# Down projections by Strassen: which of VectorE and GpSimd forms the sums of activations and weights

## What is computed

```python
D_MODEL, SEQ, DEPTH = 1024, 1024, 2
D_FF = 2816
ALPHA = (2.0 * DEPTH) ** 0.25

def swiglu(x, w_gu, w_down):
    gate, up = jnp.split(x @ w_gu, 2, axis=-1)
    return (jax.nn.silu(gate) * up) @ w_down

x = layer_norm(ALPHA * h + swiglu(h, ffn_w_gu[l], ffn_w_down[l]), ln_g[l, 1], ln_b[l, 1])
```

## Time and profile before

| what | value |
|---|---|
| median of three runs | 3269.45 us |
| the profiled execution, its own time | 3274.18 us |
| its span | 3272.5 us |
| TensorE busy (matmul) | 2939.8 us, 90% |
| VectorE busy | 1775.2 us, 54% |
| ScalarE busy | 1204.3 us, 37% |
| GpSimd busy | 1040.3 us, 32% |
| first to last matmul of the steps in `ffn0d` | 1659.4 to 1927.1 us |
| first to last matmul of the steps in `ffn1d` | 2986.7 to 3244.1 us |

### The profile page before, as it was taken

The page is one execution under the profiler, slowest core; times in us unless marked ns, Lnnn a source line. Parts: engine busy times, 40 slices in busy tenths (PEclk is TensorE's granted clock), DMA queues, the critical chain, the costliest instruction groups (busy, mean ns, idle before and its releaser), DMA issues. The chain is left out here.

```text
span 3272.5 us, 50986 instructions
## 1 busy us (share of the span) xinstructions
PE 2939.8 (90%) x18874; PEld 2460.4 (75%) x18893; DVE 1775.2 (54%) x3186; ACT 1204.3 (37%) x2655; POOL 1040.3 (32%) x1097
## 2 busy tenths in 40 slices
PE   7999999678999869999989969869996999998995
PEld 7889777354566569999977759836664999997784
DVE  2168443484898463333359873324546333334988
ACT  2222543433555443333333441114444333333342
POOL 2200222440111024444346534400001444443555
PEclk8999887788999989999999979959998999999998
DMA  4211102443110022222173432230001222226343
GB/s 124 74 41 42 27 27 76 135 125 101 48 39 27 20 65 80 80 80 80 54 244 105 162 103 40 66 112 23 27 27 53 79 80 80 80 67 207 120 160 119
DMA packets 269998, 269.61 MB, mean 82 GB/s; under 512 B 61779, under 2 KB 197158, under 8 KB 269734
## 3 DMA queue, kind: packets, MB, share of 16 engines
q1 hardware_dynamic: 263254, 255.57, 25.1%
q0 software_dynamic: 6512, 10.89, 1.1%
HBM read 212.24 MB, written 55.89 MB: 82 GB/s over the span
## 5 line engine op out<-in xcount | busy, mean ns | idle before, releaser
L2228 PE MATMUL ffn0u_ps<-ffn0u_x_hi,ffn0u_whi 128*128 128x272 f32 x1232 | 358.8, 291 | 20.4 <-DVE ffn0u_wlo L2331 10.6
L2228 PE MATMUL ffn1u_ps<-ffn1u_x_hi,ffn1u_whi 128*128 128x272 f32 x1232 | 358.4, 291 | 20.0 <-DVE ffn1u_wlo L2331 10.9
L2228 PE MATMUL ffn0u_ps<-ffn0u_x_hi,ffn0u_wlo 128*128 128x272 f32 x1232 | 356.4, 289 | 0.0
L2228 PE MATMUL ffn1u_ps<-ffn1u_x_hi,ffn1u_wlo 128*128 128x272 f32 x1232 | 356.2, 289 | 0.0
L221 PE MATMUL ine_ps<-ine_w_hi,ine_x_hi 128*128 128x256 f32 (+2 forms) x864 | 262.0, 303 | 5.2 <-DVE ine_w_lo L237 5.0
L2228 PEld LDWEIGHTS ffn0u_ps<-ffn0u_x_hi,ffn0u_whi 128*128 128x128 f32 x1232 | 234.6, 190 | 22.5 <-DVE ffn0u_wlo L2331 21.2
L2228 PEld LDWEIGHTS ffn1u_ps<-ffn1u_x_hi,ffn1u_whi 128*128 128x128 f32 x1232 | 234.2, 190 | 22.2 <-DVE ffn1u_wlo L2331 20.9
L221 PE MATMUL ine_ps<-ine_w_hi,ine_x_lo 128*128 128x256 f32 (+2 forms) x864 | 249.4, 289 | 0.0
L221 PE MATMUL ine_ps<-ine_w_lo,ine_x_hi 128*128 128x256 f32 (+2 forms) x864 | 248.9, 288 | 0.0
L2228 PEld LDWEIGHTS ffn0u_ps<-ffn0u_x_hi,ffn0u_wlo 128*128 128x128 f32 x1232 | 234.4, 190 | 0.0
L2228 PEld LDWEIGHTS ffn1u_ps<-ffn1u_x_hi,ffn1u_wlo 128*128 128x128 f32 x1232 | 234.4, 190 | 0.0
(11 more groups left out here) (559 smaller groups left out, 7902.5 us busy)
## 6 DMA issues: line engine op xcount, KB each, us to landing
ffn0u_raw<-in_ffn_w_gu_dram SPq DMA_DIRECT2D x44, 512.0 KB, 5.1
ffn0d_w<-in_ffn_w_down_dram SPq DMA_DIRECT2D x88, 256.0 KB, 2.9
ffn1u_raw<-in_ffn_w_gu_dram SPq DMA_DIRECT2D x44, 512.0 KB, 5.4
ffn1d_w<-in_ffn_w_down_dram SPq DMA_DIRECT2D x88, 256.0 KB, 3.0
scratch_a<-ffn0u_u SPq DMA_DIRECT2D x44, 272.0 KB, 2.1
scratch_a<-ffn1u_u SPq DMA_DIRECT2D x44, 272.0 KB, 2.1
aT<-scratch_a SPq DMA_DIRECT2D x8, 1024.0 KB, 10.8
aT<-scratch_a SPq DMA_DIRECT2D x10, 768.0 KB, 9.2
```

The source lines that it names most:

```text
L2228: last = nc.tensor.matmul(ps[:, bank + h, 0:TOK2], wp, xp, start=(begins and k == 0 and n == 0), stop=(k == KH - 1 and n == 2), skip_group ...
```

## The change

VectorE now makes all 55 sums of activations, and the sums of weights of products 0 and 4 (22), so one sum in every step. GpSimd keeps the sums of weights of products 2, 3 and 6 (33). VectorE's sums for step n + 1 stand ahead of the low parts of step n; ahead of step 0 stand those of step 0 and of step 1. Semaphores are renamed and counted to match.

```diff
     def dve_sums_a(n):
-        return n in a_sum_at and n in w_sum_at and n % KH2 % 2 == 0
+        return n in a_sum_at
+
+    def dve_sums_w(n):
+        return n in w_sum_at and n not in a_sum_at
+
+    w_sum_count, w_made = {}, {True: 0, False: 0}
+    for n in w_sum_steps:
+        w_made[dve_sums_w(n)] += 1
+        w_sum_count[n] = w_made[dve_sums_w(n)]
...
-        def sum_w(eng, op, n):
+        def sum_w(eng, op, n, done):
             slot, f = raw_at[n] % RW, FACTOR_B[n // KH2]
             eng.wait_ge(w_in[slot], w_in_count[n])
             second = raw2[:, pair_at[n] % 2, :] if n in pair_at else b22(n % KH2)
-            op.tensor_tensor(raw[:, slot, :], raw[:, slot, :], second, f[1]).then_inc(w_sum_done, 1)
+            op.tensor_tensor(raw[:, slot, :], raw[:, slot, :], second, f[1]).then_inc(done, 1)
+
+        def wait_w_sum(eng, n):
+            eng.wait_ge(w_sum_dve if dve_sums_w(n) else w_sum_pool, w_sum_count[n])
...
                             if q == 1 and pair_at[n] >= 2:
-                                sp.wait_ge(w_sum_done, w_sum_at[pair_steps[pair_at[n] - 2]] + 1)
+                                wait_w_sum(sp, pair_steps[pair_at[n] - 2])
...
                     if n in w_sum_at:
-                        act.wait_ge(w_sum_done, w_sum_at[n] + 1)
+                        wait_w_sum(act, n)
...
                     if n in a_sum_at:
-                        act.wait_ge(a_sum_dve if dve_sums_a(n) else a_sum_pool, a_sum_count[n])
+                        act.wait_ge(a_sum_dve, a_sum_count[n])
...
             def _(pool):
                 for n in range(STEPS):
-                    if n in w_sum_at:
-                        sum_w(pool, nc.gpsimd, n)
-                    if n in a_sum_at and not dve_sums_a(n):
-                        sum_a(pool, nc.gpsimd, n, a_sum_pool)
+                    if n in w_sum_at and not dve_sums_w(n):
+                        sum_w(pool, nc.gpsimd, n, w_sum_pool)
...
                 for n in range(STEPS):
-                    if n + 1 < STEPS and dve_sums_a(n + 1):
-                        sum_a(dve, nc.vector, n + 1, a_sum_dve)
+                    for m in (n, n + 1):
+                        if m < STEPS and (m == n + 1 or n == 0):
+                            if dve_sums_w(m):
+                                sum_w(dve, nc.vector, m, w_sum_dve)
+                            if dve_sums_a(m):
+                                sum_a(dve, nc.vector, m, a_sum_dve)
                     dve.wait_ge(w_hi_done, n + 1)
```

More of the change, by code:

```diff
@@ L2487, in ffn_down @@
         x_first, x_right, x_left0, x_left1, x_sample = (sem(n) for n in ("x_first", "x_right", "x_left0", "x_left1", "x_sample"))
-        w_sum_done, a_sum_pool, a_sum_dve = sem("w_sum_done"), sem("a_sum_pool"), sem("a_sum_dve")
+        w_sum_pool, w_sum_dve, a_sum_dve = sem("w_sum_pool"), sem("w_sum_dve"), sem("a_sum_dve")
         w_hi_done, w_split, a_hi_done, a_split = sem("w_hi_done"), sem("w_split"), sem("a_hi_done"), sem("a_split")
@@ L2591, in _ @@
                         if k == 3:
-                            sp.wait_ge(w_sum_done, w_sum_at[4 * KH2 - 1] + 1)
+                            wait_w_sum(sp, 4 * KH2 - 1)
                         load_group(a21_in, GROUPS2, (k - 3) // 2, A21)
```

## The result

The changed kernel takes 3279.5 us in the median of 22 runs (3273.3 to 3292.8), the kernel before 3270.2 us in 22 runs beside it: a ratio of 1.0030, 95% interval 1.0018 to 1.0042. It is slower by 0.3%, where 3261 was forecast and 3248 to 3272 was the range. The profiled execution has a span of 3279.7 us, 7.2 more than before.

The account below looks back on a forecast made before the run. TensorE was taken as the limit except where VectorE, full in products 2 and 3, made late adds and three waits. Terms 2.9 - 3.6 - 2.5 + 0 - 1.0 = -4.2 a stage, -8.4 for both: 3261 against 3269.45; range 3248 to 3272.

Parts of the forecast that it names:

- Product 4: Product 4: TensorE bound, with pairs of loads giving 2.3 us a step; change 0, at most +1 at its first steps.
- Rival C: Products 0, then 4: a late load blocks finished low parts; +5 us a stage at load time 7.4; chance 0.08.
- Start of product 0: First matmul: VectorE makes step 1's sum before the low parts of step 0; +2.9 us.
- Rest of product 0: Product 0 after its start: loads allow 3.1 us a step, just under TensorE's 3.20; cost 0, bounds 0 and +7.
- First step of product 1: Product 1's first step: the 2.15 us wait vanishes, with the clock's part; -3.9, taken as 3.6, bounds -4 and 0.
- Products 2 and 3: Between adds of products 1 and 2: 38.0 us becomes 36.4, adds come 2.5 earlier; -2.5, bounds -0.3 and -6.
- The price of 1.10: Each GpSimd sum that meets VectorE's SBUF work holds VectorE back by 1.78 - 0.68 = 1.10 us.
- Products 5 and 6: From product 4's adds to the last low part: -1.0 us a stage in sum, bounds -5 and +2.
- the estimate beside the forecast: With full blocking a GpSimd sum costs VectorE 1.3; the five leaving products 2 and 3 give 1 us more a stage.
- Rival B: VectorE just stays full: products 2 to 6 gain nothing, start and first wait cancel; 3268 us; chance 0.17.
- Rival A: Adds of products 2 and 5 come 5 to 6 us earlier, waits shrink, clock holds; about -12 a stage, 3246; chance 0.20.

Follow-up runs that it names:

- a21_later: The changed kernel with the three loads of A21 issued two steps later each: 3276.1 us, ratio to the kernel before 1.0020.
- a21_two: The changed kernel with two groups of A21 (2 MB) issued at product 4's k = 3, the third at k = 7: 3291.1 us in one run.
- late: The changed kernel with VectorE's weight sum of step n + 1 made last in step n: 3263.5 us, ratio to the kernel before 0.9973.
- p4_pool: The changed kernel with the weight sums of product 4 given back to GpSimd: 3269.2 us, ratio to the kernel before 0.9995.
- start: The changed kernel with step 1's weight sum behind the low parts of step 0: 3280.1 us, ratio to the kernel before 1.0038.
- late_all: As late, with every weight sum on VectorE: 3240.9 us, ratio to the kernel before 0.9908; again 3241.3 us, 0.9914.
- mid: late_all with A21 loaded two steps later and product 4's weight sums between the low parts of the step in front: 3237.2 us, 0.9913.
- swap_only: The kernel before with only 15 sums of activations a stage (products 2, 3, 6) moved from GpSimd to VectorE: 3267.2 us, ratio 0.9998.

## Why the prediction was wrong

**The step that failed** is "*Product 4.* TensorE bound; pairs of loads take 2.9 in the median ... **0**, at most +1 at its first steps." It cost 7.0 us in each stage. The median of 2.9 is over all 88 weight loads; the one load that mattered had 1 MB of A21 ahead of it, and 7.5 us passed from its first issue to the sum. Before the change it was 7.2. So it could have been read from the trace of before, as GpSimd's sum of step 48 shows. The step also looked at TensorE's pace through product 4, and not at what else waited in VectorE's stream behind that sum: the adds of product 3, which TensorE needs 2.0 us into the product. `a21_later`, `a21_two` and `late` show both halves of it.

It was not the only miss. A stage was forecast at -4.2 and came to +3.9 and +7.2; product 4 is 7.0 of the 8.1 and 11.4 between. And `p4_pool`, which is the change without that cost, ends at 3269.2 and not at 3261: the gains forecast ahead of product 4 did not come either.

Rival C had this mechanism, with a chance of 0.08, but put it in product 0, with product 4 named only in brackets, and priced it as a pace: it would decide from a load time of 7.4 us on. In truth one load of that length at the step ahead of the adds was enough.

Point by point, in us a stage (`ffn0d`, `ffn1d`):

- *Start of product 0*: forecast +2.9, measured +2.2 and +3.1. Right as a term; by `start`, though, taking it away alone does not shorten the kernel.
- *Rest of product 0*: forecast 0, measured -0.3 and -0.4. TensorE waits nowhere in it. Right.
- *First step of product 1*: forecast -3.6, measured -2.1 and +0.2. The adds came later than my replay had them; counted from the start of the stage they began at 52.1 and 53.1 us, where they were forecast at 51.2 (1700.3, less the 1649.15 at which TensorE fell idle ahead of the stage). VectorE stood at loads here too. VectorE's timeline in `ffn1d` shows it at the load of step 10 and at the first block of A12:

```profile
3015.75 0.69 DVE L2532 TENSOR_TENSOR ffn1d_w<-ffn1d_w,aT 128x512 f32<-128x512 f32 x1 [3.42 <-DMA aT<-in_ffn_w_down_dram]
...
3019.41 0.69 DVE L2544 TENSOR_TENSOR ffn1d_a_sum<-aT 128x512 f32<-128x512 f32 x1 [1.76 <-DMA aT<-scratch_a]
```

  I had taken 4.3 us for that load; from the issue of its B22 tile (3009.02) to the sum it was 6.7, with two tiles of X issued just ahead. `late` takes product 1 to 35.2 and 35.6. How much of the two numbers is the change and how much the noise of product 1 is not shown.
- *Products 2 and 3*: forecast -2.5, measured -1.1 and -0.5. The adds of product 1 did start earlier against the product's end, at 0.07 instead of 0.79. But the distance to the next adds stayed at 37.9 (38.2 in `ffn1d`), where I had 36.4. Ten GpSimd sums met VectorE rather than nine, 1.1 us more, and my sum had left out an add of the sample tokens' result that stands in this stretch, 0.6 (for before, it was hidden in the 1.0 of "small waits"):

```profile
1753.84 0.67 DVE L2785 SCALAR_TENSOR_TENSOR ffn0d_X<-ffn0d_X,ffn0d_ps 64x512 f32<-64x512 f32 x1
```

  The price of 1.10 for a sum that meets VectorE held roughly: 1.79 against 0.68 in the rows above, and 1.54 to 1.79 over all 14 such operations of this stretch before.
- *Products 5 and 6*: forecast -1.0, measured -1.9 and -2.2. Right in sign, half in size.

By the Trainium skill (SBUF — State Buffer, "Who interferes with whom") whoever has the shared port pair holds it for the whole instruction, and the other fully blocks. By the estimate beside the forecast that would have put it 2 us lower and so a little more wrong; by these rows the price stays at 1.10 and not 1.3. The Trainium skill's page Perfetto Trace Analysis ("Optimizing Scalar/DVE Operations") says that offloading from a saturated VectorE, even to GpSimd, may make sense, and warns that between those two it might not help. The runs agree with the warning: the two fastest kernels, `late_all` and `mid`, offload no sum at all.

Rival B, that VectorE stays full, was right for products 2 to 3, and `swap_only` agrees; product 6 gained all the same. Rival A, that the waits shrink to 1 or 2 and the clock stays up, was not what this change did, but is near what `late_all` does, by taking GpSimd out altogether: the granted clock is 1.00 in its windows of products 3 and 6, and 0.96 in product 4.

## What to carry to other kernels

In this kernel an operation that waits for a transfer did not belong ahead of work whose operands were ready, on an engine that also frees the banks for the next product. Look for such a place, try the operation last in the step, and price it with the one load that is late there and what waits behind it, not with the median. Where two engines hold each other up, count what a piece of work costs on both: a GpSimd sum that costs VectorE 1.10 us is worse than VectorE's own at 0.60, but of the kernels tried only the ones without any such sum in products 2 and 3 brought the step under TensorE's pace.

## What the runs showed that I had not expected

- A one for one exchange at 1.10 against 0.60 was worth nothing measurable (`swap_only`, 0.9998), though on paper it saves 0.5 us each. Between the adds of products 1 and 2 of `ffn0d` VectorE has 5 operations more and 10 stretched ones instead of 14. At 0.60 and 0.2 of waiting for the low part in front, the five cost 4.0; four stretched ones fewer give back 4.4. In `late_all` the weight sum stands between the two; the step there is 2.59 for four operations.
- The weight tiles of 256 KB behind 1 MB on the same queue landed 5.0 to 7.2 us after their own issue, over the tiles of step 48 in both stages before and after the change, against 2.9 in the median.
